# Gates of the dense pair of token blocks: one-hot products replaced by a scattered add into DRAM

## The chip, the cores and the metric

The kernel runs on one core of one Trainium2 chip. The metric is device time in microseconds (us) of one execution; before the change the median of three runs is 5275.13 us.

## The reference, cut to what matters

Two layers work on 768 tokens of width 1024, 256 of context and 512 latent, in six blocks of 128. A layer is a mixer (recurrence and two kinds of attention) and then a retrieval feed-forward over 16384 experts of one neuron each; the last layer does it for the four latent blocks only. The change is in the feed-forward:

```
q = (hb @ wq).reshape(PEER_BLOCK, PEER_HEADS, 2, PEER_DK // 2)
s = jnp.einsum('thpd,hpnd->thpn', q, subkeys)
top_s, top_i = lax.top_k(s, PEER_TOPK)              # 16 of 128, twice a head
best_s, pos = lax.top_k(cand_s, PEER_TOPK)          # 16 of the 16 x 16 sums
idx = jnp.take_along_axis(cand_i, pos, axis=-1)
g = jax.nn.softmax(best_s, axis=-1)
a = gelu(einsum('td,thkd->thk', hb, u_tab[idx]))
out = einsum('thk,thkd->td', g * a, v_tab[idx])
```

Each token chooses 16 experts in each of 8 heads, 128 in all, with a gate for each. Two heads of a token may choose the same expert; their gates then add.

## The kernel before, in words

Five engines run programs of their own, tied by semaphores: PE (matmuls), ACT, DVE, POOL and SP, which issues the large loads. At the end of each stage `stage_end` makes PE, ACT, DVE and POOL wait for one another; SP runs through.

The blocks of a layer go through the feed-forward in two ways. A **gathered** pair of blocks (`gathered_passes`) takes the products with all experts, in 128 chunks of 128 experts: PE makes h times u (`up_gathered`, L1277, split in two fp32r parts for accuracy, or `up_plain`, L1259, every other chunk of layer 0's second pass), ACT applies gelu (L1685) and SP stores the 128 x 128 x 256 result in DRAM (`hx`, L497). For the split chunks ACT copies the high part of u (L1677) and DVE subtracts for the low part (`low_gathered`, L2501). Later POOL gathers for each token its chosen activations (`take_activations`, L671, one instruction for each of the 128 choices of a block, one element for each partition) and its 128 rows of v (`take_row`, L677, 4 KB for each partition), and DVE adds the weighted rows (`add_row`, L2471). In layer 0 one block's rows are added beside the second products pass (`beside_products`), the other three beside the dense stage (`beside_dense`); in layer 1 both beside the dense stage. A plan (`row_plan`) says after which chunk which row is due.

The **dense** pair is the last one, blocks 4 and 5. It makes both products over all 128 chunks: up (L1352), gelu (L1795), times a matrix of gates G (DVE, L2638), down (L1361 plain in layer 0, L1376 split in layer 1). SP streams one ring tile of 1 MB a chunk (u and v), four slots, each free after the down product of its chunk.

G (expert by token, zero where a token has not chosen) is 128 KB a partition of SBUF. It is built in a stage of its own, `gbuild`: for each token DVE makes one-hot matrices of the row and column of its choices (L2598, L2589, L2594), ACT or DVE weighs them with the gate (L1751, L2594), PE multiplies them to the token's 128 x 128 gates (L1331), and ACT copies them to G (L1756). Beside it POOL gathers 64 activations and in layer 0 fetches 3 rows.

The order in a layer: queries of the first pair; its products pass, in which DVE does the top-k work of that pair (`retrieve`, a few steps after each chunk, ready at chunk 44) and at chunk 60 the queries of the next pair; in layer 0 a second products pass (blocks 2, 3) with the queries of blocks 4, 5 after chunk 16 and the added rows of block 0; `gbuild`; the dense stage. In layer 1 there is one products pass (blocks 2, 3). ACT and POOL take part in the choice by the softmax exponent (`gates`) and by storing the gates in DRAM (`gx`, L698). Where indices of one pair would be overwritten they are parked in DRAM (`ix`), and so is the sum of block 0 (`ys`).

## Time and profile before

| | |
|---|---|
| runs | 5266.3, 5275.13, 5329.87 us; median 5275.13 |
| profiled execution | 5303.6 us, span 5301.9 us |
| busy | PE 88%, PE weight load 73%, DVE 59%, POOL 34%, ACT 29% |
| DMA | 1103.74 MB, mean 208 GB/s |

A row by stage gives the busy time of each engine in that stretch, the number of its instructions in brackets, the clock that TensorE was granted (1.00 is full), the mean busy share of the 16 DMA engines and what they moved. The stages of layer 0, by their start in us: queries 810, first products pass 874, second 1331 (queries in it at 1410), build 1945, dense 2063 to 3101; of layer 1: queries 3755, products 3828 (queries in it at 4010), build 4271, dense 4447 to 5280. fp32 matmuls stand as two records each.

### The profile page before, as it was taken

Reading aid. Unit: us, or ns where it says so; the run is one execution under the profiler, and the core shown is the slowest. Engines: PE = TensorE matmul, PEld = TensorE weight load, DVE = VectorE, ACT = ScalarE, POOL = GpSimd, SP = SyncE. Lnnn points to the kernel's source line nnn. Section 1 sums busy time; section 2 is a strip of 40 time slices with the busy share of each in tenths; the row PEclk is TensorE's granted clock in tenths of the full one; section 3 lists DMA queues with packets and bytes.
Section 4 is the critical chain, followed back from the end, with each engine's and each line's share of the span. In section 5 each row is a group of like instructions: output and inputs, shape, how many; then the busy total and the mean of one; then the engine's idle time right before and its main releaser. Section 6 shows DMA issues by size and latency. Waiting matters only on the chain.

```text
span 5301.9 us, 75651 instructions
## 1 busy us (share of the span) xinstructions
PE 4666.2 (88%) x25798; PEld 3895.4 (73%) x25798; DVE 3121.5 (59%) x6247; ACT 1525.4 (29%) x2757; POOL 1827.7 (34%) x1918
## 2 busy tenths in 40 slices
PE   8889899999788876898998987799999948999998
PEld 6569788999777765555555665588899947778886
DVE  2673646666356656454554655646576736667777
ACT  2333422534212233000000023334253425222322
POOL 1111210000456557666666411113000041666652
PEclk9989999999889989999999998799999969999999
DMA  4331115656479863888998942212365722889997
GB/s 150 112 104 54 31 72 177 223 176 211 145 259 321 304 219 123 316 320 317 335 334 330 371 173 79 79 62 66 131 215 177 226 77 76 318 321 339 359 356 267
DMA packets 316699, 1103.74 MB, mean 208 GB/s; under 512 B 59392, under 2 KB 108672, under 8 KB 267872
## 3 DMA queue, kind: packets, MB, share of 16 engines
q1 hardware_dynamic: 165024, 648.09, 35.1%
q0 software_dynamic: 151488, 453.35, 23.9%
q8 instruction: 93, 1.52, 0.1%
q14 instruction: 94, 0.77, 0.0%
HBM read 1037.13 MB, written 62.03 MB: 207 GB/s over the span
## 4 chain that ended last, share of the span: by engine, by line
PE 69%; issue 9%; another core or an unknown queue 7%; DVE 7%; ACT 4%; POOL 2%; POOLq 1%; DMA 1%; ACTq 0%; DVEq 0%; PEldq 0%; SPq 0%
PE PS L1277 16%; PE PS L1352 14%; PE PS L1361 7%; PE PS L1376 6%; PE PS L1222 5%; PE PS L939 3%; PE PS L937 3%; PE PS L1259 3%; PE PS L1180 3%; PE PS L1019 2%; POOL arena L671 1%; PE PS L998 1%; DVE PS L2471 1%; PE PS L1076 1%
## 5 line engine op out<-in xcount | busy, mean ns | idle before, releaser
L1277 PE MATMUL PS<-hS,wS 128*128 128x256 f32 x7680 | 974.5, 289 | 92.4 <-ACT wS L1677 69.1
L1277 PEld LDWEIGHTS PS<-hS,wS 128*128 128x128 f32 x7680 | 954.2, 196 | 109.4 <-issue 80.4
L671 POOL DMA_INDIRECT arena<-hx,arena x768 | 788.5, 1027 | 630.6 <-POOLq L406 333.0
L1352 PE MATMUL PS<-hS,ring 128*128 128x256 f32 x4096 | 954.4, 384 | 51.5 <-issue 41.4
L1352 PEld LDWEIGHTS PS<-hS,ring 128*128 128x128 f32 x4096 | 786.4, 192 | 233.2 <-issue 119.4
L2501 DVE TENSOR_TENSOR wS<-ring,wS 128x1024 fp32r<-128x1024 f32 x320 | 392.0, 1225 | 469.0 <-ACT wS L1677 382.3
L677 POOL DMA_INDIRECT arena<-in_experts,arena x465 | 480.7, 1034 | 515.1 <-DVE PS L2471 392.5
L2471 DVE SCALAR_TENSOR_TENSOR PS<-arena,PS 128x1024 f32<-128x1024 f32 x462 | 593.4, 1284 | 26.3 <-DMA arena<-in_experts,arena 13.2
L1361 PE MATMUL PS<-ring,arena 128*128 128x512 f32 x1024 | 488.1, 622 | 61.2 <-DVE arena L2638 53.8
L1795 ACT ACTIVATE arena<-PS 128x256 f32<-128x256 f32 x256 | 97.3, 384 | 1280.7 <-PE PS L1352 776.9
L2638 DVE TENSOR_TENSOR arena<-arena 128x256 f32<-128x256 f32 x256 | 108.8, 425 | 533.8 <-ACT arena L1795 354.6
L1376 PE MATMUL PS<-wS,gS_ 128*128 128x512 f32 x1536 | 403.1, 412 | 16.0 <-DVE gS_ L2642 13.1
L1361 PEld LDWEIGHTS PS<-ring,arena 128*128 128x128 f32 x1024 | 202.9, 200 | 276.7 <-issue 208.8
L2471 DVE SCALAR_TENSOR_TENSOR PS<-spare,arena,PS 128x1024 f32<-128x1024 f32 x300 | 385.9, 1286 | 28.0 <-DMA spare<-in_experts,arena 6.4
L1685 ACT ACTIVATE arena<-PS 128x256 f32<-128x256 f32 x384 | 147.5, 384 | 787.6 <-PE PS L1277 466.9
L677 POOL DMA_INDIRECT spare<-in_experts,arena x303 | 291.9, 963 | 217.7 <-DVE PS L2471 141.3
L1376 PEld LDWEIGHTS PS<-wS,gS_ 128*128 128x128 f32 x1536 | 292.8, 191 | 83.0 <-DVE gS_ L2642 15.9
L1677 ACT ACTIVATE wS<-ring 128x1024 fp32r<-128x1024 f32 x320 | 336.6, 1052 | 11.3 <-DMA ring<-in_experts 8.2
L1259 PE MATMUL PS<-arena,ring 128*128 128x256 f32 x1024 | 246.0, 392 | 31.4 <-issue 21.2
L1259 PEld LDWEIGHTS PS<-arena,ring 128*128 128x128 f32 x1024 | 195.9, 197 | 65.0 <-issue 27.7
L1222 PE MATMUL PS<-arena,ring 128*128 128x256 f32 x1024 | 230.4, 384 | 11.8 <-DMA ring<-in_wq 11.8
L698 POOL DMA_DIRECT2D gx<-arena x6 | 3.4, 568 | 673.3 <-DVE arena L2111 377.3
(331 smaller groups left out, 6299.4 us busy)
## 6 DMA issues: line engine op xcount, KB each, us to landing
ring<-in_experts SPq DMA_DIRECT2D x256, 1024.0 KB
ring<-in_experts SPq DMA_DIRECT2D x384, 512.0 KB
ring<-in_wcat SPq DMA_DIRECT2D x80, 1024.0 KB
hx<-arena SPq DMA_DIRECT2D x384, 128.0 KB
ring<-in_wq SPq DMA_DIRECT2D x40, 1024.0 KB
arena<-in_rpb POOLq DMA_DIRECT2D x96, 128.0 KB, 2.6
arena<-hx,arena POOLq DMA_INDIRECT x768
arena<-xs POOLq DMA_DIRECT2D x20, 512.0 KB, 5.6
```

Of the source, the lines that this page charges most:

```text
L671: pool.indirect_dma_start(out=aX[n][:, k:k + 1], out_offset=None, in_=src, in_offset=bass.IndirectOffsetOnAxis(ap=at[:, k:k + 1], axis=0)) ...
L677: pool.indirect_dma_start(out=dst, out_offset=None, in_=d["experts"].rearrange("l c p (h f) -> (l c p h) f", h=2), in_offset=bass.Indirect ...
L937: return pe.matmul(bank[n % 4][:, 0:end_ - at], w[:, m * P:(m + 1) * P], h[:, k, at:end_], start=start, stop=stop)
L1222: mm = pe.matmul(bank[n % 4][:, 0:PASS], w[:, m, k, :], tokens[:, k, :], start=(k == 0), stop=(k == KD - 1))
L1259: mm = pe.matmul(bank[6 + c % 2][:, 0:PASS], u[:, k, :], hP[:, k, :], start=(k == 0), stop=(k == KD - 1))
L1277: mm = pe.matmul(bank[6 + c % 2][:, 0:PASS], u[:, k, :], hS[:, h, k, :], start=(part == 0 and k == 0), stop=(part == 2 and k == KD - 1))
L1352: mm = pe.matmul(bank[c % 2][:, 0:PASS], u[:, k, :], hS[:, 0, k, :].bitcast(F32), start=(k == 0), stop=(k == KD - 1))
L1361: mm = pe.matmul(bank[4 + 2 * tb + h], gel[2 + c % 2][:, tb * P:(tb + 1) * P], ring[:, sl, D + 512 * h:D + 512 * h + 512], start=start, st ...
L1376: mm = pe.matmul(bank[4 + 2 * tb + h], gS_[:, 2 * (c % 2) + g, tb * P:(tb + 1) * P], wS[:, 2 * (c % 2) + v, 512 * h:512 * h + 512], start= ...
L1677: act.activation(wS[:, 2 * (c % 2) * (per == 1), :], ring[:, c % SLOTS, 0:D], ACT.Copy).then_inc(s["xu_hi"], 1)
L2471: op = dve.scalar_tensor_tensor(out=total, in0=row, scalar=aX[n][:, k:k + 1], in1=total, op0=ALU.mult, op1=ALU.add)
L2501: dve.tensor_tensor(wS[:, at + 1, :], ring[:, c % SLOTS, 0:D], wS[:, at, :].bitcast(F32), ALU.subtract).then_inc(s["slot_free"], 1)
```

## The change

The dense pair becomes the first one asked: blocks 0 and 1 in layer 0, 2 and 3 in layer 1; the gathered passes are the two others (one in layer 1). There is no `gbuild` stage, no one-hot matrix and no G in SBUF.

Its gates go to a matrix `gd` in DRAM (16.8 MB, chunk, expert, token). SP fills it with zeros during attention, 16 DMAs of 1 MB from a zeroed tile. After the choice DVE makes each chosen element's address (`chosen`), and POOL adds the gates there, one indirect DMA with `compute_op=add` for each of 128 choices and 2 blocks (`scatter`): seven of eight heads in layer 0's first products pass and the last in the second, all eight in layer 1's pass. Each head waits for the same block's head before it to have landed. In the dense stage SP loads 128 KB of gates with each ring tile (`Gb`, four slots), and DVE waits for them.

The normalized tokens of the dense pair are kept in DRAM (`hd`) until the dense stage. Those of the first gathered pair are made within the first queries. The retrieval of the dense pair runs at 2.0 steps a chunk instead of 1.25, before chunk 32, where now the next queries stand; the second pass has its queries after chunk 16 as before. Row buffers are free from the start of the dense stage, so the plan is simpler; rows begin after chunk 2 in layer 0 and chunk 9 in layer 1. All activations but the 64 gathered in layer 0's second pass are gathered in the dense stage (320 in layer 0, 256 in layer 1), the first 16 in layer 0 and 40 in layer 1 ahead of the rows. The parking of indices and of one sum in DRAM falls away, and the token blocks lie elsewhere in SBUF.

The diff, cut to its core:

```diff
-    return range(first_block(layer), NB - 2, 2)
+    return range(first_block(layer) + 2, NB, 2)
+def first_pass(layer, f):
+    return f == first_block(layer) + 2
+def queries_at(layer, f):
+    return 8 if first_pass(layer, f) else 4
...
-    return 11 if f == first_block(layer) else 0
-def queries_at(layer, f):
-    return norm_after(layer, f) + 4
+    return queries_at(layer, f) + 2 if f + 2 < NB else None
 def gates_at(layer, f):
-    return queries_at(layer, f) + (10 if f == first_block(layer) else 12)
+    return queries_at(layer, f) + (10 if first_pass(layer, f) else 12)
...
-        G = view(0, PK, PASS)
         KT0 = 32768
-        kT = view(KT0, 3, PASS)
...
+        eD = arena[:, KT0:KT0 + 2 * P].bitcast(U32).rearrange("p (b k) -> p b k", b=2)
+        gD = view(KT0 + 2 * P, 2, P)
+        Gb = view(23552, SLOTS, PASS)
...
+            def dense(l):
+                base = tally["tiles"]
+                def load(i, sl):
+                    sp.dma_start(ring[:, sl, :], d["experts"][l][bass.ds(i * SLOTS + sl, 1), :, :].rearrange("o p f -> p (o f)")
+                                 ).then_inc(w_ready[sl], 16)
+                def gates(i, sl):
+                    sp.dma_start(Gb[:, sl, :], gd[bass.ds(i * (SLOTS * P * PASS) + sl * P * PASS, P * PASS), :]
+                                 .rearrange("(p t) o -> p (t o)", t=PASS)).then_inc(g_in[sl], 16)
...
+                for tb in range(2):
+                    sp.wait_ge(scattered[tb], 16 * P * (l + 1))
+                for sl in range(SLOTS):
+                    gates(0, sl)
+                with sp.Fori(1, PK // SLOTS) as i:
+                    for sl in range(SLOTS):
+                        sp.wait_ge(s["down_done"], i * SLOTS + (l * PK + sl - SLOTS + 1))
+                        load(i, sl)
+                        gates(i, sl)
...
+                sp.wait_ge(s["zeros_made"], l + 1)
+                size, at_unit = PK * P * PASS // 16, (0 if l == 0 else 12 * len(units(0)))
+                for i in range(16):
+                    sp.wait_ge(s["exp_done"], 1 + at_unit + 2 * i)
+                    sp.dma_start(gd[i * size:(i + 1) * size, :].rearrange("(p t) o -> p (t o)", p=64),
+                                 k8[64:128, 0:size // 64]).then_inc(s["zero_out"], 16)
...
+                def scatter(heads):
+                    for h in heads:
+                        for tb in range(2):
+                            if h:
+                                pool.wait_ge(scattered[tb], 16 * (P * l + TOPK * h))
+                            for k in range(TOPK * h, TOPK * (h + 1)):
+                                pool.indirect_dma_start(out=gd, out_offset=bass.IndirectOffsetOnAxis(ap=eD[:, tb, k:k + 1], axis=0),
+                                                        in_=gD[:, tb, k:k + 1], in_offset=None, compute_op=ALU.add
+                                                        ).then_inc(scattered[tb], 16)
...
+                    if first_pass(l, f):
+                        if f + 2 < NB:
+                            pool.wait_ge(s["hd_out"], 16 * (l + 1))
+                            pool.wait_ge(s["pq_done"], 16 * t["pass"])
+                            load_pass(f + 2)
+                        pool.wait_ge(s["gates_ready"], l + 1)
+                        scatter(range(HEADS if l + 1 == DEPTH else HEADS - 1))
                     else:
-                        pool.dma_start(ix[0], eB.rearrange("p b k -> p (b k)")).then_inc(s["ix_out"], 16)
-                        pool.dma_start(ix[1], vB.rearrange("p b k -> p (b k)")).then_inc(s["ix_out"], 16)
+                        store_gates(f - 2)
                         pool.dma_start(gX[3], gx[l, f0]).then_inc(s["gx_in"], 16)
+                        scatter([HEADS - 1])
...
-                built = min(P, ahead + BUILT)
-                take_activations(0, late[0], range(ahead, built))
-                due, buf, prev = row_plan(len(late), buffers_free(l))
-                held = HELD if early else 0
-                for r in range(held):
-                    take_row(vX[l][buf[r]], buf[r], vA[:, late[0] % 2], r)
-                end(f"gbuild{l}{b0}")
...
+                    groups(1, meet, 0)
                     t["tiles"] = base + meet * SLOTS
-                    queries(hQ if some_plain(l, f) else hP)
+                    queries(hP)
...
-                    def gates_of(i, first):
-                        for g in range(GD):
-                            pe.wait_ge(s["row_made" if g % 2 else "rows_ready"], i * (GD // 2) + (gb // 2 + g // 2 + 1))
-                            if not first:
-                                pe.wait_ge(s["g_used"], i * GD + (gb + g + 1 - GD))
-                            for q in range(4):
-                                mm = pe.matmul(bank[4 + g][:, q * P:(q + 1) * P], oneA[g][:, q, :],
-                                               oneB[g][:, q, :].bitcast(F32), start=True, stop=True)
-                            mm.then_inc(s["one_used"], 1)
...
-                    def weigh_group(i, g):
-                        act.wait_ge(s["one_ready"], i * (GD // 2) + (gb // 2 + g // 2 + 1))
-                        if not isinstance(i, int) or i:
-                            act.wait_ge(s["one_used"], i * GD + (gb + g + 1 - GD))
-                        for q in range(4):
-                            at = arena[:, bass.ds(i * (4 * GD) + (KT0 + 2 * PASS + 4 * g + q), 1)]
-                            last = act.activation(oneA[g][:, q, :], oneR[g][:, q, :].bitcast(F32), ACT.Identity, scale=at)
-                        last.then_inc(s["rows_ready"], 1)
-                    def copy_out(i, g):
-                        act.wait_ge(s["one_used"], i * GD + (gb + g + 1))
-                        act.activation(G[:, :, bass.ds(i * (4 * GD) + 4 * g, 4)],
-                                       bank[4 + g].rearrange("p (t j) -> p j t", j=P), ACT.Copy
...
+                for tb in range(2):
+                    act.wait_ge(scattered[tb], 16 * P * (l + 1))
...
+                def chosen():
+                    dve.wait_ge(s["sel_ready"], 2 * t["pass"])
+                    for tb in range(2):
+                        last = dve.scalar_tensor_tensor(out=eXD[:, tb], in0=sels[tb][:, 1, :], scalar=float(P),
+                                                        in1=sels[tb][:, 0, :], op0=ALU.mult, op1=ALU.add)
+                    link(last)
+                    for tb in range(2):
+                        last = dve.tensor_scalar(eFD[:, tb], eXD[:, tb], float(PASS), pcol[:, tb:tb + 1], ALU.mult, ALU.add)
+                    link(last)
+                    for tb in range(2):
+                        dve.tensor_copy(eD[:, tb], eFD[:, tb])
+                        last = dve.tensor_copy(gD[:, tb], sels[tb][:, 2, :])
+                    last.then_inc(s["gates_ready"], 1)
...
-                        own = retrieve(t["pass"], 0, 4 * FIRST_GATES + 1)
...
-                            some_steps(own, c, 1.25)
+                            some_steps(own, c, 2.0)
                         for _ in own:
                             pass
                         t["pass"] += 1
-                        indices(True)
+                        chosen()
...
-                                dve.tensor_tensor(oneB[g], iota[:, :].unsqueeze(1).broadcast_to([P, 4, P]),
-                                                  at[:, 1].unsqueeze(2).broadcast_to([P, 4, P]), ALU.is_equal)
-                                for n in range(4):
-                                    own, gate = (arena[:, bass.ds(i * (4 * GD) + (KT0 + v * PASS + 4 * g + n), 1)]
-                                                 for v in (0, 2))
-                                    last = dve.tensor_scalar(oneA[g][:, n, :], iota[:, :], own, gate,
-                                                             ALU.is_equal, ALU.mult)
...
-                        dve.tensor_tensor(gel[2 + c % 2], gel[c % 2], G[:, c, :], ALU.mult).then_inc(s["gfull"], 1)
...
+                    dve.wait_ge(g_in[c % SLOTS], 16 * (l * PK // SLOTS + c // SLOTS + 1))
+                    dve.tensor_tensor(gel[2 + c % 2], gel[c % 2], Gb[:, c % SLOTS, :], ALU.mult).then_inc(s["gfull"], 1)
...
```

## Rows read from the trace of the kernel before

**Rows 1.** The page: the chain that ended last, by line (share of the span).

```profile
PE PS L1277 16%; PE PS L1352 14%; PE PS L1361 7%; PE PS L1376 6%; PE PS L1222 5%; PE PS L939 3%; PE PS L937 3%; PE PS L1259 3%; PE PS L1180 3%; PE PS L1019 2%; POOL arena L671 1%; PE PS L998 1%; DVE PS L2471 1%; PE PS L1076 1%
```

**Rows 2.** Busy time by stage: us, busy (x instructions) per engine, clock, DMA share, GB/s.

```profile
874.00:1331.00 457.00, 442.94 (x3438) 434.25 (x3438) 317.30 (x869) 214.89 (x318) 6.93 (x12) 0.99 0.65 207
1476.00:1945.00 469.00, 390.79 (x2218) 350.42 (x2217) 284.40 (x410) 97.97 (x171) 262.76 (x257) 0.91 0.86 297
1945.00:2063.00 118.00, 68.75 (x516) 62.32 (x515) 92.41 (x194) 71.99 (x192) 85.00 (x67) 0.92 0.16 56
2063.00:3101.00 1038.00, 938.73 (x3072) 599.41 (x3072) 546.01 (x533) 48.14 (x128) 621.35 (x651) 0.95 0.88 323
3828.00:4271.00 443.00, 434.66 (x3392) 425.72 (x3391) 309.24 (x850) 209.16 (x312) 1.15 (x2) 1.00 0.64 203
4271.00:4447.00 176.00, 74.86 (x512) 68.42 (x512) 91.88 (x193) 72.58 (x192) 64.00 (x64) 0.76 0.09 31
4447.00:5280.00 833.00, 808.27 (x3584) 682.58 (x3584) 572.72 (x652) 233.37 (x384) 477.94 (x456) 0.99 0.87 321
```

**Rows 3.** The same view, three stretches in which PE runs undisturbed.

```profile
2999.00:3051.00 52.00, 52.00 (x182) 34.39 (x181) 35.43 (x35) 2.69 (x7) 22.33 (x23) 1.00 0.98 378
5123.00:5175.00 52.00, 52.00 (x236) 44.37 (x235) 39.48 (x45) 15.96 (x25) 17.63 (x18) 1.00 0.95 348
1126.00:1320.00 194.00, 193.63 (x1614) 193.43 (x1613) 137.80 (x295) 93.25 (x138) 0.00 (x0) 1.00 0.69 219
```

**Rows 4.** Instructions in order of time, PE, layer 0's second pass: start, us, instruction.

```profile
1387.32 3.61 PE L1259 MATMUL PS<-arena,ring 128*128 128x256 f32 x16
1393.64 3.61 PE L1259 MATMUL PS<-arena,ring 128*128 128x256 f32 x16
```

**Rows 5.** Busy time in layer 0's queries of the second pass.

```profile
1410.00:1476.00 66.00, 65.70 (x347) 58.73 (x346) 39.68 (x265) 12.23 (x27) 31.35 (x33) 1.00 0.38 124
```

**Rows 6.** Busy time in two stretches with gathers of single activations.

```profile
1353.00:1378.00 25.00, 5.17 (x18) 3.85 (x18) 2.64 (x3) 3.67 (x6) 12.89 (x14) 0.52 0.13 35
4271.00:4360.00 89.00, 21.90 (x112) 20.20 (x112) 22.72 (x47) 15.24 (x40) 64.00 (x64) 0.58 0.18 61
```

**Rows 7.** Instructions in order of time, PE: last products, first dense ones.

```profile
1938.72 3.61 PE L1259 MATMUL PS<-arena,ring 128*128 128x256 f32 x16
...
2063.09 3.36 PE L1352 MATMUL PS<-hS,ring 128*128 128x256 f32 x7 [8.61 <-POOLq L406]
...
4265.72 4.00 PE L1277 MATMUL PS<-hS,wS 128*128 128x256 f32 x32
...
4447.08 7.17 PE L1352 MATMUL PS<-hS,ring 128*128 128x256 f32 x32 [0.72 <-ACTq L406]
```

**Rows 8.** DMA issues: KB each, us from issue to landing.

```profile
hS<-hQ SPq DMA_DIRECT2D x1, 1024.0 KB, 5.3
```

**Rows 9.** Busy time of layer 1's first pass up to its choice.

```profile
3828.00:3956.00 128.00, 125.73 (x1042) 124.94 (x1042) 106.92 (x265) 71.19 (x99) 0.84 (x2) 1.00 0.70 220
```

**Rows 10.** The page: instructions, busy us, mean ns; idle us, releaser.

```profile
L2501 DVE TENSOR_TENSOR wS<-ring,wS 128x1024 fp32r<-128x1024 f32 x320 | 392.0, 1225 | 469.0 <-ACT wS L1677 382.3
```

**Rows 11.** Busy time in layer 0's attention.

```profile
500.00:716.00 216.00, 188.43 (x1242) 166.13 (x1241) 129.55 (x400) 103.47 (x253) 57.75 (x78) 0.96 0.13 37
```

**Rows 12.** Instructions in order of time, POOL: gathers in the two build stages.

```profile
2000.32 1.63 POOL L671 DMA_INDIRECT arena<-hx,arena  x1 [0.30 <-issue]
...
2003.50 1.60 POOL L671 DMA_INDIRECT arena<-hx,arena  x1 [0.31 <-issue]
...
4308.48 0.95 POOL L671 DMA_INDIRECT arena<-hx,arena  x1 [0.30 <-issue]
4309.73 0.95 POOL L671 DMA_INDIRECT arena<-hx,arena  x1 [0.30 <-issue]
```

**Rows 13.** One line: times ns (min/median/max), first and last start.

```profile
L671 POOL DMA_INDIRECT arena<-hx,arena x768: 946/952/2007, 1328.4 to 5096.8; - x192
...
L677 POOL DMA_INDIRECT arena<-in_experts,arena x465: 937/945/2007, 1476.0 to 5259.6; - x155
```

More of the change, by code:

```diff
@@ L117, in rows_due @@
         for c in range(PK):
-            have = sum(not f or f + lead <= c for f in free)
-            at += min(step, have / 2 + 0.5) if have else 0
+            at += min(step, buffers / 2 + 0.5) if c >= start else 0
             due.append(min(total, int(at)) if c < PK - 1 else total)
@@ L125, in row_plan @@
         step += 1 / 64
[L126 to L135 removed]
+    return rows_due(step), [r % buffers for r in range(total)]
 class Chain:
@@ L316, in build @@
         xl = view(XL, 2, D)
+        hD = view(XL, KD, PASS)
         xf = view(4096, 4, D)
@@ new lines, in group @@
+                def group(i, first, last):
+                    for sl in range(SLOTS):
+                        if sl < SLOTS - 1:
+                            up(i, sl + 1, sl + 1)
+                        elif not last:
+                            up(i + 1, 0, 0)
+                        down(i, sl, sl, first and sl == 0, last and sl == SLOTS - 1)
+                pe.wait_ge(s["h_in"], 16 * (ps_ + 1))
+                up(0, 0, 0)
+                group(0, True, False)
+                with pe.Fori(1, PK // SLOTS - 1) as i:
+                    group(i, False, False)
@@ new lines, in _, with v_high @@
+                ps_ = t.get("dense", 0)
+                cb = ps_ * PK
+                t0 = t["tiles"]
+                sb_ = sum(split_rows(m) for m in range(l)) * PK
+                def v_high(i, c, first=False):
+                    sl = c % SLOTS
+                    act.wait_ge(w_ready[sl], (i + c // SLOTS) * 16 + 16 * (t0 // SLOTS + 1))
+                    if not (first and c < 2):
+                        act.wait_ge(s["down_done"], i * SLOTS + (cb + c - 1))
+                    act.activation(wS[:, 2 * (c % 2), :], ring[:, sl, D:2 * D], ACT.Copy).then_inc(s["v_hi"], 1)
```

707 lines of the change are left out of this document (298 added, 409 removed).

## The prediction

> **What bounds the kernel now.** I read the chain of waits first, then the busy time by stage, then the instructions around each stage boundary. The chain says that TensorE (PE) sets the end: its lines for the gathered products (L1277), the dense up product (L1352) and the dense down products (L1361, L1376) lead it, and no other engine has more than 1% on one line [rows 1]. Cut by stage, PE is nearly full in each layer's first products pass (443 of 457 and 435 of 443 us), less so in layer 0's second pass (391 of 469) and its dense stage (939 of 1038), and almost full in layer 1's dense stage (808 of 833). Between them stand the two gate-building stages, where PE works 69 of 118 us and 75 of 176 us, on one-hot products alone [rows 2]. The critical resource of everything else, PE at its pace, is given by three undisturbed stretches: 182 matmul records in 52 us, 24 to a dense plain chunk, so 6.86 us a chunk; 236 records, 28 to a split chunk, so 6.17 us; 1614 in 194 us, 24 to a gathered chunk, so 2.88 us [rows 3]. A plain and a split chunk of layer 0's second pass take 6.32 us together [rows 4].
>
> Against that pace four stretches lose time, and each of them has POOL gathering single activations (one 4-byte element for each partition) from DRAM: the second pass of layer 0 (1331 to 1942 less 66 us of queries [rows 5] and 64 x 6.32 leaves 141 us, with 192 gathers by the code), layer 0's dense stage (1038 - 128 x 6.86 = 160 us, 256 gathers), layer 1's dense stage (833 - 128 x 6.17 = 43 us, 192 gathers), and the build of layer 1, which takes 58 us longer than that of layer 0 with the same work and the same 64 gathers [rows 2, 6]. In two stretches where POOL issues nothing but such gathers PE does 5.2 of 25 us and 21.9 of 89 us while DMA is 13 to 18% busy [rows 6]. When only row fetches are left, PE loses nothing [rows 3]. So a gather costs 0.73, 0.62, 0.22 and about 0.9 us of PE, and in the build of layer 0 none that I can see. The smaller costs go with a busier VectorE (DVE): 0.61, 0.53, 0.69 of the time, and 0.78 in layer 0's build [rows 2]. Why, the trace does not show; the change adds 512 instructions of this kind.
>
> **The change part by part.**
> *The build stages go.* From the last product to the first dense product it is 1942.3 to 2063.1 and 4269.7 to 4447.1, so 121 + 177 = 298 us [rows 7]. What stays is a boundary: the 1 MB copy of h lands in 5.3 us [rows 8], then the first 1 MB tile (2.8 us at the 378 GB/s of [rows 3]), and some 4 us of barrier, formerly beside the build. The first gate tiles queue behind five megabytes, 14 us, but the first two up products (7 us) run meanwhile. I take 14 us a layer (9 if the barrier hides, 30 at worst, the length of the dead stretch in rows 6). Removed net: 298 - 28 = 270.
>
> *Gate loads.* 128 loads of 128 KB a layer, 16.8 MB. Full DMA is 378 / 0.98 = 386 GB/s, so 44 us of all engines. The dense stages use 0.88 x 1038 = 913 and 0.87 x 833 = 725 us of DMA; with the loads 957 and 769, still below the 0.98 at which PE ran full [rows 2, 3]. Hidden on average, not in every moment: I take 20 us a layer, between 0 and 44. The added DVE wait comes right behind a ring tile issued three chunks, 20 us, earlier; behind it stand the row additions, and PE and ACT wait for its product.
>
> *Gathers that lose their stage.* 64 a layer (and 3 row fetches) move into the dense stages. At those stages' rates 64 x 0.62 + 64 x 0.22 = 54 us; nothing, if the loss goes with the hour and not the gather; I take 27. POOL has room: 704 instructions x 1.32 us = 929 of 1038 us.
>
> *Retrieval pressed together.* The first choice now ends before chunk 32 instead of 44. DVE has 107 us of work in the 128 us to the choice [rows 9], 44 x 1.22 = 54 of it weight splits [rows 10]; the other 53 plus 26 splits (32) and the links between them make about 100 us, where PE wants 26 x 2.88 = 75. PE is slowed for part of it, as it already loses 3 us there: 5 us a layer, 10 together, at most 30, at least 0. The choice then comes 100 us into the pass instead of 128; with 3 us of index arithmetic (eight small instructions) the scatters start at 977 and 3931.
>
> *Scatters.* 256 a layer: 7 heads (224) in layer 0's first pass, 32 in the second, 256 in layer 1's only pass. No row shows a DMA that adds into DRAM. The nearest are the gathers, with the same 128 elements: in the second pass 257 such instructions are 263 us busy plus 0.30 between them, 1.32 us each [rows 2]. Ends: 977 + 224 x 1.32 = 1273, before the pass ends at about 1331 + 5 = 1336; 3931 + 256 x 1.32 = 4269, before 4271 + 5 = 4276. So POOL's issue is covered, narrowly in layer 1; past it every 0.1 us costs 26 us. The waits from head to head have 16 instructions, 21 us, of the other block between them: nothing. The 32 left over (42 us) delay the end of the first 32 gathers from 1373 to 1415, and the next wait for query products that begin at 1410 anyway [rows 5]: nothing. What the scatters do to PE is the disputed term: 0 to 0.73 us each. The first passes have DVE at 0.69 to 0.70, like the dense stage of layer 1 [rows 2], so I take its 0.22: 512 x 0.22 = 113 us, ends 0 and 374.
>
> *Zeros, and the rest.* 16.8 MB a layer are written in attention, where DMA is 13% busy [rows 11]; 44 us in 216, cover enough. SP waits there, with only weight tiles behind it that wait for later slots. Uncovered it would be 44 us a layer. The norm moves from products to queries at equal size; POOL's copy of h and DVE's 3 us of indices replace stores and transposes of the same size: 0.
>
> Sum: 270 - 40 - 27 - 10 - 113 = 80 us off. The profiled execution took 5303.6 us (span 5301.9), 28 above the median of 5275.1; 80 off it is 5224, off the median **5195 us**.
>
> What an adding DMA costs, a page bears on. The Trainium skill, Collectives: The Full Stack (the bandwidth ceiling), says that a reduce needs two source reads, hence twice the read descriptors of a copy. No run here shows it; if it held for POOL's instruction, the sum would be that of rival 3.
>
> **The rivals.**
> 1. *No disturbance*: DVE keeps POOL from crowding, as in layer 0's build. 270 - 77 = 193 off, **5082**. For: PE lost nothing with 32 gathers in the queries at 1410 [rows 5]. Chance 0.22.
> 2. *DVE slows the scatters*: with DVE at 0.78 gathers come 1.59 us apart, without it 1.25 [rows 12]. At 1.59: layer 0 ends at 1333 (covered), layer 1 at 3931 + 407 = 4338 (+62); 193 - 62 = 131 off, **5144**. Chance 0.12. The Trainium skill, GPSIMD Engine Reference (Specifications), states that POOL shares its SBUF interfaces with DVE and contends with DVE instructions of two SBUF inputs; rows 12 agree with it.
> 3. *The scatter is the slower instruction* (the other side): if its busy part doubles, 2 x 1.02 + 0.30 = 2.34 us, POOL ends layer 0's pass at 1501 (+165) and layer 1's at 4530 (+254): 193 - 419, **5501**. It decides where (193 + 359 + 345) / 480 = 1.87 us an instruction is passed, 359 and 345 being the time that the two passes give 480 scatters. For: nothing here shows an add at a DMA's target. Against: an instruction that gathers 4 bytes a partition and one that fetches 4 KB take 0.952 and 0.945 us in the middle [rows 13], so the size of the work hardly shows. Chance 0.13.
> 4. *Heavy disturbance*, 0.73 each: 193 - 374, **5456**. Against: the second pass has less DVE work. Chance 0.12.
> 5. *The dense stages turn DMA-bound*: 88 and 54 instead of 40 and 27, with the 113: 5 off, **5270**. Chance 0.08.
> The change doing something else than it says has no place: the one-hot code is gone.
>
> **How the numbers follow.** The forecast, 5195, has 0.33, its own range 5150 to 5240. Two per cent, about what a measurement of this kernel can tell, is 5170 and 5381. Faster: rival 1, most of 2 and a third of the forecast, 0.41. Slower: rivals 3 and 4 with a small tail, 0.26. Same: 0.33. The range runs from 5060, just under rival 1, to 5410; rivals 3 and 4 lie mostly above it, which leaves out about 0.2.
>
> **What would show it.** Right: no stage between products and dense, the first dense product some 14 us after the last gathered one; scatters 1.3 us apart, done before PE in both first passes; dense stages of 1078 and 860 us; first passes 60 us longer, with PE idle beside an idle DMA. Rival 1: first passes unchanged. Rivals 2 and 3: PE and ACT waiting for POOL at the end of the pass. Wrong altogether if the scatters' completion, not their issue, holds POOL at the head-to-head waits, or if attention grows.

## The result and the profile after

The changed kernel takes **5653.9 us** in the median of four runs (5641.8 to 5666.2) beside 5302.5 us of the kernel before (four runs, 5266.3 to 5337.2): ratio 1.066, 95% interval 1.057 to 1.076. The forecast was 5195, range 5060 to 5410. The profiled executions, 5646.7 and 5303.6 us, are 343 us apart where I had 80 the other way.

The page after. First the chain that ended last, by line, then two of its groups (line, engine, operation, out<-in, count | busy us, mean ns | idle before, releaser):

```profile
POOL gd L709 15%; PE PS L1340 12%; PE PS L1349 6%; PE PS L1364 5%; PE PS L1292 3%; PE PS L937 3%; PE PS L935 3%; PE PS L1274 3%; PE PS L1192 2%; PE PS L1234 2%; PE PS L1031 2%; PE PS L1010 1%; DVE wS L2484 1%; POOLq L401 1%
...
L1340 PE MATMUL PS<-hS,ring 128*128 128x256 f32 x4096 | 1000.1, 393 | 337.5 <-POOLq L401 190.4
...
L709 POOL DMA_INDIRECT gd<-arena x512 | 912.5, 1782 | 439.8 <-DVE arena L2467 281.2
```

The scatter, L709, which did not exist before, now leads the chain that PE's products led [rows 1]. By stage, in the columns of [rows 2]: layer 0's first pass and its tail, its second pass with the queries, its dense stage, layer 1's mixer, pass, tail and dense stage:

```profile
889.00:1349.00 460.00, 444.45 (x3417) 431.50 (x3416) 319.22 (x899) 233.56 (x333) 303.38 (x162) 0.99 0.78 200
1349.00:1478.00 129.00, 0.30 (x1) 0.33 (x2) 2.64 (x2) 3.13 (x3) 102.73 (x67) 0.52 0.27 18
1478.00:2124.00 646.00, 524.27 (x2880) 469.14 (x2879) 334.83 (x691) 140.28 (x233) 382.16 (x354) 0.88 0.74 245
2129.00:3276.00 1147.00, 970.85 (x3072) 613.73 (x3072) 547.18 (x533) 48.29 (x128) 680.61 (x717) 0.91 0.86 310
3276.00:3966.00 690.00, 560.44 (x3359) 476.04 (x3358) 351.46 (x793) 241.38 (x420) 112.37 (x161) 0.88 0.33 97
4042.00:4490.00 448.00, 438.91 (x3384) 426.37 (x3384) 309.32 (x856) 222.24 (x313) 297.92 (x155) 1.00 0.79 202
4490.00:4680.00 190.00, 0.00 (x0) 0.00 (x0) 0.00 (x0) 0.27 (x1) 156.71 (x102) 0.51 0.30 29
4680.00:5624.00 944.00, 842.09 (x3584) 692.39 (x3584) 571.76 (x653) 231.30 (x385) 547.30 (x522) 0.94 0.83 302
```

The passes are as long as before (460 and 448 against 457 and 443), but two stretches of 129 and 190 us follow in which PE, DVE and ACT do nothing and only POOL works. The end of the second one, in order of time:

```profile
4638.81 1.55 POOL L709 DMA_INDIRECT gd<-arena  x1 [0.30 <-issue]
4640.66 1.55 POOL L709 DMA_INDIRECT gd<-arena  x1 [0.30 <-issue]
...
4675.90 1.55 POOL L709 DMA_INDIRECT gd<-arena  x1 [0.30 <-issue]
4678.92 1.75 SPq L456 DMA_DIRECT2D arena<-gd  x4
...
4680.26 4.21 PE L1340 MATMUL PS<-hS,ring 128*128 128x256 f32 x9 [190.41 <-POOLq L401]
```

A scatter is 1.55 us busy and 0.30 apart, 1.85 us with nothing beside it; a gather takes 0.95 and 0.30 [rows 12]. And the dense stages take 1147 and 944 us where they took 1038 and 833 [rows 2].

### The profile page after: what moved, and what is told of

Same layout as the page of the kernel before. It is cut to its first block, busy times and chain, and to the rows that moved or that the text cites. A ratio compares the mean times of both kernels' runs of the same rounds, so it can differ in the third digit from the quotient of the medians.

```text
span 5645.0 us, 72801 instructions
## 1 busy us (share of the span) xinstructions
PE 4630.4 (82%) x24762; PEld 3814.6 (68%) x24762; DVE 2939.8 (52%) x5875; ACT 1437.5 (25%) x2419; POOL 2716.5 (48%) x2422
## 4 chain that ended last, share of the span: by engine, by line
PE 47%; POOL 16%; issue 12%; DVE 10%; another core or an unknown queue 10%; ACT 3%; POOLq 1%; DMA 1%; ACTq 0%; DVEq 0%; PEldq 0%; SPq 0%
POOL gd L709 15%; PE PS L1340 12%; PE PS L1349 6%; PE PS L1364 5%; PE PS L1292 3%; PE PS L937 3%; PE PS L935 3%; PE PS L1274 3%; PE PS L1192 2%; PE PS L1234 2%; PE PS L1031 2%; PE PS L1010 1%; DVE wS L2484 1%; POOLq L401 1%
## 5 line engine op out<-in xcount | busy, mean ns | idle before, releaser
L1340 PE MATMUL PS<-hS,ring 128*128 128x256 f32 x4096 | 1000.1, 393 | 337.5 <-POOLq L401 190.4
L1340 PEld LDWEIGHTS PS<-hS,ring 128*128 128x128 f32 x4096 | 802.4, 197 | 546.1 <-issue 240.1
L1292 PE MATMUL PS<-hS,wS 128*128 128x256 f32 x7680 | 986.4, 290 | 218.1 <-ACT wS L1674 174.1
L709 POOL DMA_INDIRECT gd<-arena x512 | 912.5, 1782 | 439.8 <-DVE arena L2467 281.2
L685 POOL DMA_INDIRECT arena<-hx,arena x768 | 763.7, 994 | 250.0 <-issue 231.7
L2484 DVE TENSOR_TENSOR wS<-ring,wS 128x1024 fp32r<-128x1024 f32 x320 | 392.2, 1225 | 588.1 <-ACT wS L1674 500.7
L2434 DVE SCALAR_TENSOR_TENSOR PS<-arena,PS 128x1024 f32<-128x1024 f32 x465 | 597.3, 1284 | 15.9 <-issue 2.1
L1349 PE MATMUL PS<-ring,arena 128*128 128x512 f32 x1024 | 500.7, 635 | 82.6 <-DVE arena L2583 71.6
L2583 DVE TENSOR_TENSOR arena<-arena 128x256 f32<-128x256 f32 x256 | 108.7, 425 | 705.3 <-ACT arena L1756 520.5
L2434 DVE SCALAR_TENSOR_TENSOR PS<-spare,arena,PS 128x1024 f32<-128x1024 f32 x297 | 382.0, 1286 | 22.4 <-DMA spare<-in_experts,arena 1.0
L2556 DVE TENSOR_TENSOR wS<-ring,wS 128x1024 fp32r<-128x1024 f32 x128 | 156.9, 1226 | 347.2 <-ACT wS L1749 269.0
L1234 PE MATMUL PS<-arena,ring 128*128 128x256 f32 x1280 | 296.8, 389 | 37.2 <-issue 25.5
L1234 PEld LDWEIGHTS PS<-arena,ring 128*128 128x128 f32 x1280 | 246.5, 195 | 75.1 <-issue 42.7
```

Source lines behind the costliest of these rows:

```text
L685: pool.indirect_dma_start(out=aX[n][:, k:k + 1], out_offset=None, in_=src, in_offset=bass.IndirectOffsetOnAxis(ap=at[:, k:k + 1], axis=0)) ...
L709: pool.indirect_dma_start(out=gd, out_offset=bass.IndirectOffsetOnAxis(ap=eD[:, tb, k:k + 1], axis=0), in_=gD[:, tb, k:k + 1], in_offset=N ...
L1234: mm = pe.matmul(bank[n % 4][:, 0:PASS], w[:, m, k, :], tokens[:, k, :], start=(k == 0), stop=(k == KD - 1))
L1292: mm = pe.matmul(bank[6 + c % 2][:, 0:PASS], u[:, k, :], hS[:, h, k, :], start=(part == 0 and k == 0), stop=(part == 2 and k == KD - 1))
L1340: mm = pe.matmul(bank[c % 2][:, 0:PASS], u[:, k, :], hS[:, 0, k, :].bitcast(F32), start=(k == 0), stop=(k == KD - 1))
L1349: mm = pe.matmul(bank[4 + 2 * tb + h], gel[2 + c % 2][:, tb * P:(tb + 1) * P], ring[:, sl, D + 512 * h:D + 512 * h + 512], start=start, st ...
```

## The experiments

Each is the changed kernel with one edit, unless it says otherwise.

**A surprise first: the chips differ.** The experiments ran on five chips. On four of them the kernel before takes 4922 to 4925 us, and the changed one, run on one of these, 5191; on the fifth it takes 5296 and the changed one 5620, about as in the first runs (whose chip may be the same one). I call the four *quiet*, the fifth and that of the first runs *disturbed*, and compare numbers of one chip or of quiet chips. The fifth also spreads more: its 13 runs of the kernel before go from 5233.9 to 5370.6 us.

**r_before, r_after: both kernels on a quiet chip.**

> The kernel before, unchanged, for a profile from the chip of the experiments. There its median was 4923 us instead of 5275. If the excess of the first chip is in the stretches where POOL gathers (second pass, dense stages, build of layer 1), these are 350 us shorter here and the undisturbed first passes, mixers and queries as long as before; the gathers then disturb nothing here. If it is the clock (0.970 against 0.944 granted), all stages are shorter in proportion to PE's share.

> The changed kernel, unchanged, on the chip of the experiments. Theory A alone (tails of 127 and 186 us against the removed 298, and small dense-stage costs that are the same on every chip): 4923 + 20 to 60 us for tails less build, plus gate loads and a longer attention, some 4990 to 5250. Without its 248 gate loads it took 5194 here, so with them it should take 5195 to 5220 if they are hidden, 5250 and more if not.

Measured: 4923.0 us (4916.5 to 4929.6) and 5190.8 (5189.9 to 5194.6), ratio 1.054 (1.052 to 1.056). The kernel before, its second pass behind the queries, dense stage 0, build 1, dense stage 1 on the quiet chip:

```profile
1446.00:1815.00 369.00, 358.95 (x2243) 332.91 (x2242) 284.95 (x415) 102.12 (x172) 276.29 (x259) 1.00 0.99 378
1935.00:2813.00 878.00, 877.82 (x3058) 582.82 (x3059) 548.92 (x533) 49.03 (x128) 613.43 (x651) 1.00 0.98 382
3992.00:4103.00 111.00, 68.46 (x519) 62.20 (x517) 92.58 (x194) 72.33 (x193) 82.03 (x64) 0.97 0.14 49
4103.00:4895.00 792.00, 789.58 (x3561) 672.93 (x3562) 568.89 (x644) 236.02 (x382) 468.67 (x456) 1.00 0.92 338
```

They stand against 469, 1038, 176 and 833 us in [rows 2]. These windows of the quiet chip end some 6 us before the last product of each dense stage; taken from product to product, the four differ by 98, 154, 66 and 31 us, and 25 more lie in the second pass ahead of its queries (53 us here, 78 there). That is 374 of the 375 us between the two profiled spans: the difference between the chips lies in the stretches with gathers and nowhere else. The changed kernel there, dense stage 0, the tail and dense stage 1 of layer 1:

```profile
1998.00:2953.00 955.00, 899.81 (x3056) 577.81 (x3055) 541.22 (x532) 48.80 (x127) 679.20 (x716) 0.99 0.98 372
...
4173.00:4363.00 190.00, 0.00 (x0) 0.00 (x0) 0.00 (x0) 0.34 (x1) 156.83 (x102) 0.51 0.29 29
4363.00:5156.00 793.00, 791.61 (x3561) 674.37 (x3561) 569.05 (x643) 236.02 (x382) 530.39 (x522) 1.00 0.95 359
```

The tail is the same 190 us on either sort of chip; dense stage 1 costs nothing here (793 for 792), dense stage 0 costs 77.

**e1 and e2: the price of the scatter.** In e1 a gather stands in the scatter's place, in e2 the scatter does not add (both on a quiet chip):

```
- indirect_dma_start(out=gd, out_offset=...(eD[:, tb, k:k + 1]), in_=gD[:, tb, k:k + 1], in_offset=None, compute_op=ALU.add)
e1: indirect_dma_start(out=gD[:, tb, k:k + 1], out_offset=None, in_=gd, in_offset=...(eD[:, tb, k:k + 1]))
e2: indirect_dma_start(out=gd, out_offset=...(eD[:, tb, k:k + 1]), in_=gD[:, tb, k:k + 1], in_offset=None)
```

> Each of the 512 adding scatters is replaced by a gather of one element for each partition from the same matrix, by the same indices, into the gate columns (so the gates are never scattered: the dense pair gets gates of zero). Theory A (the scatter is the slower POOL instruction: 1.55 us busy and 0.30 between against 0.95 and 0.30 of a gather): the gathers come 1.25 to 1.35 us apart, POOL ends layer 0's first pass at 996 + 224 x 1.35 = 1298, before the products end at 1349, and layer 1's at 4144 + 256 x 1.35 = 4490 instead of 4677; the tails of 127 and 186 us go, and the kernel takes some 5340 to 5360 us. Rival (POOL's time is the number of DMAs in flight or of completions, whatever their kind): 1.85 us apart and the tails stay, 5640. Second rival (gathers, unlike scatters, disturb the other engines): tails gone, but the two first passes grow by 0.2 to 0.6 us a gather, 100 to 300 us in all, 5450 to 5600.

> The scatters write instead of adding (a gate chosen by two heads for one token is then lost; nothing else changes). If the add is what costs POOL 0.6 us more than a gather, the scatters take 0.95 us and the result is as with gathers, some 5340 to 5360 us. If it is the direction (a scattered write of 128 elements, each a descriptor of its own into DRAM), they stay at 1.55 us and the kernel at 5640 to 5660; the DMA share in the tail (0.22 and 0.29) then falls only if the add costs the DMA engines something.

Measured: 4889.1 us (4887.1 to 4895.1) and 4898.3 (4896.3 to 4902.0), where the changed kernel takes 5190.8: 302 and 293 us off. One line each, times in ns (minimum/median/maximum), e1 and then e2:

```profile
L709 POOL DMA_INDIRECT arena<-gd,arena x512: 944/948/1972, 999.1 to 4056.2; - x171
```

```profile
L709 POOL DMA_INDIRECT gd<-arena x512: 964/971/2004, 996.5 to 4070.3; - x171
```

Of e2, the same stretch as the tail above, from the last product of layer 1 to the first dense one:

```profile
4050.00:4074.00 24.00, 0.02 (x1) 0.02 (x1) 0.00 (x0) 0.04 (x1) 16.38 (x17) 0.58 0.60 230
```

So reading or writing makes no difference (0.95 and 0.97 us); **the addition is what costs POOL 0.58 us more, 1.55 us**, and that takes the stretch from 24 to 190 us. Theory A holds; the direction is out, and so is the number of DMAs in flight. The two forecasts of 5340 to 5360 us were for the first chip, some 300 us off its 5654, and 302 and 293 is what came off on a quiet one.

The page counts the DMA's packets too, here of r_after and then of e2 (e1 has the same numbers of packets as e2):

```profile
DMA packets 429084, 1169.58 MB, mean 225 GB/s; under 512 B 137600, under 2 KB 219648, under 8 KB 377952
```

```profile
DMA packets 371740, 1169.58 MB, mean 239 GB/s; under 512 B 80256, under 2 KB 162304, under 8 KB 320608
```

With the addition there are 57,344 small packets more, 112 for each of the 512 instructions. In stretches with scatters alone the software queue shows some 34 packets for a plain one (542 for 16 in e2) and some 145 for an adding one (13,466 for 93 in r_after). POOL's time and its packets grow together; that the one makes the other no run shows.

**e3: the gate loads.** Of 128 loads a layer four are left (`gates(i, sl)` is taken out of the loop, VectorE waits for the first ones only).

> Only the first four gate tiles of a layer are loaded in the dense stages; the other 124 chunks take old tiles of gates (248 loads of 128 KB, 32.5 MB, are left out, with VectorE's waits for them). Theory B1 (the dense stages are 109 and 111 us longer because of the gate loads on the DMA engines and in SP's queue): they come back to 1040 to 1060 and 835 to 850 us, 5450 to 5480 in all. Theory B2 (they are longer because of the gathers moved into them and the 40 that open layer 1's): 0 to 40 us off, 5610 to 5650, and the first 104 us of layer 1's dense stage still have POOL full and PE at half.

Measured: 5194.3 us (5193.4 to 5195.9), the changed kernel 5190.8: nothing. The loads are hidden on the quiet chip, and B1 is out there. On the disturbed chip e8 below, which keeps all the loads, has dense stages as short as the quiet chip's, so they cost nothing there either.

**e8: the gathers of the dense stages**, on the disturbed chip, beside the unchanged kernel there:

```
- rest = [(n, k) for n in ... for k in range(..., P)]
+ rest = [(n, k) for n in ... for k in range(..., P) if k % 32 == 31]
```

> The changed kernel again, beside the following ones on the same chip: 5191 us if it is the chip of the last runs, 5654 if it is one like the first. In the second case layer 1's dense stage is 931 us long again and not 793, and the following kernel, without most gathers there, tells whether it is the gathers that make it so.

> Of the 320 and 256 gathers of single activations that the dense stages issue, only one in 32 stays (those rows are then weighted with old numbers). Layer 0's dense stage took 955 us against 878 of the kernel before on the same chip, without any gain from leaving the gate loads out. Theory P (POOL is its bound: 704 instructions x 1.35 = 950 us, and VectorE, which makes the gates' products in order behind the row additions, waits for the rows): it comes back to 878 us, PE's pace; layer 1's, with 512 instructions, stays at 793; 5191 - 77 = 5114. Rival (the DMA engines, 0.98 busy, are its bound): 310 gathers of 512 bytes are too little to matter, it stays above 940, and the kernel above 5175.

Measured: 5619.9 us (5611.7 to 5635.7) and 5242.7 (5236.5 to 5260.3), 377 off. Dense stages 0 and 1 of the changed kernel on this chip, then of e8:

```profile
2134.00:3269.00 1135.00, 971.99 (x3057) 612.22 (x3057) 546.80 (x533) 48.17 (x128) 681.76 (x715) 0.90 0.87 313
...
4678.00:5601.00 923.00, 833.42 (x3561) 689.24 (x3560) 562.20 (x643) 231.23 (x383) 552.17 (x522) 0.94 0.85 308
```

```profile
2118.00:2999.00 881.00, 878.12 (x3057) 582.20 (x3056) 548.69 (x532) 48.66 (x127) 378.32 (x406) 1.00 1.01 403
4413.00:5204.00 791.00, 791.00 (x3566) 674.44 (x3565) 569.82 (x644) 236.60 (x384) 269.89 (x274) 1.00 0.95 359
```

Without most gathers the dense stages of the disturbed chip are as short as a quiet chip's (881 for 878, 791 for 792); with them a gather costs 254 / 310 = 0.82 us in layer 0 and 132 / 248 = 0.53 in layer 1. The DMA engines carry more (403 GB/s) when the stage is shorter, and e3's stage 0 is as long as the changed kernel's, 963 us from first to last product, with 16 MB less to move (DMA busy 0.94 instead of 0.97), so they aren't its bound. What the other engines wait for, in dense stage 1 on the disturbed chip, PE (us in total, times, longest):

```profile
PE PS L1340 <- issue: 49.5, 45, 3.6
PE PS L1364 <- DVE gS_ L2587: 26.6, 12, 4.3
PE PS L1364 <- issue: 12.5, 8, 2.9
```

"issue" is idle time in which nothing visible is waited for; on the quiet chip this list has one wait of 1.0 us. For layer 0, 77 of the cost is there on a quiet chip too: POOL is 679 us busy in 716 instructions, with 0.30 between them 894 of 955 us, and VectorE makes the gates' products (L2583) in order behind the row additions (L2434), which wait for POOL's rows. What PE and VectorE wait for there, on the quiet chip (r_after):

```profile
PE PS L1349 <- DVE arena L2583: 54.9, 49, 9.5
```

```profile
DVE PS L2434 <- DMA spare<-in_experts,arena: 283.1, 165, 5.2
```

In 67 us POOL itself waits for VectorE to free a row buffer, so the two hold each other up, POOL far more. e9b and e13 below have 16 gathers fewer in this stage and take 947 and 943 us from first to last product instead of 963, 1.0 to 1.2 us an instruction. Theory P holds, for layer 0; its own test, e8, fell on the disturbed chip, where it takes off this bound and the disturbance together.

**e4: the zeros.** Layer 1's 16 transfers are left out (its dense pair then also has layer 0's gates).

> The zero fill of layer 1 (16 transfers of 1 MB in attention) is left out; the matrix then holds layer 0's gates too, so that layer 1's dense pair is wrong. If the fill made attention longer (layer 1's mixer took 690 us instead of 654), that stage comes back to about 655 us and the kernel is 30 to 36 us faster than the changed one. If it was hidden, nothing changes (within 5 us).

Measured: 5169.3 us (5166.3 to 5173.0), 21.5 off, neither of the two forecasts. I had put the zeros at nothing behind attention.

**e5: the kernel before, its gathers moved** (BUILT is 64 in layer 0 and 0 in layer 1, `head = 40`), on a quiet chip.

> The kernel before, with layer 1's 64 gathers of the build stage issued at the start of the dense stage (40 of them ahead of the first row instead of 16): everything else as before. If gathers slow the other engines wherever they are, the build of layer 1 shrinks from 176 to about 118 us, that of layer 0, and its dense stage grows by 50 to 60 us from 833: nothing in all, 5260 to 5310. If the dense stage hides them, 50 to 60 us are gained, 5215 to 5250, and theory B2 for the changed kernel is wrong. If the build stage was long for another reason, it stays at 176 and the whole becomes 10 to 50 us slower.

Measured: 4946.4 us (4943.2 to 4948.4) beside 4923.1, ratio 1.004 (1.003 to 1.006). None of the three, for the forecasts were for the first chip: the build stays as it was (110 us), since on a quiet chip it never suffered, and the dense stage takes 13 us more. In the profiled execution 6 us more stand before layer 0's first queries, where nothing was changed. What the move does on a disturbed chip isn't known.

**e7: layer 0's scatters divided 5 to 3** (`range(HEADS - 3)` in the first pass, the others in the second).

> Layer 0's scatters are divided 5 heads to the first pass and 3 to the second, instead of 7 and 1. At 2.0 to 2.3 us each beside a busy VectorE, the 160 scatters end at 996 + 160 x 2.15 = 1340, before the products (1349): layer 0's tail of 127 us goes. The 64 moved ones take 120 to 140 us at the head of the second pass, where POOL has its gathers and rows later: if POOL has slack there, the kernel gains 100 to 127 us; if the second pass is then bound by POOL's row fetches (0.95 us each and VectorE's 1.29), up to all of it is given back there and the kernel stays within 20 us.

Measured: 5195.7 us (5189.0 to 5196.4), nothing gained. The tail goes, the second pass becomes as much longer (519 us behind its queries instead of 396): POOL has no slack to move work into.

**e9 to e13: can it be had without the addition?** VectorE sums the gates of a token's repeated experts, and plain scatters write head by head, all 8 heads in the first pass; 80 gathers ahead instead of 64 (in the second pass, beside the 128 of the block whose rows are added there).

```
+ def merge(h, tb):            # n = TOPK * (h + 1)
+     for e in range(TOPK * h, TOPK * (h + 1)):
+         scalar_tensor_tensor(out=both[...], in0=eK[:, tb, 0:n], scalar=eK[:, tb, e:e + 1], in1=gR[:, tb, 0:n],
+                              op0=ALU.is_equal, op1=ALU.mult, accum_out=gD[:, tb, e:e + 1])
```

> A version meant to be right and fast: VectorE gives each choice of a head the sum of its own gate and those of earlier heads for the same expert (224 small instructions a layer, some 30 us, in sixteens between the chunks), so that a plain scatter, the last writer winning, does what the adding one did. All 8 heads are scattered in the first pass of layer 0 too, and 80 instead of 64 gathers are taken ahead in its second pass. By the plain scatter's 0.97 us busy, POOL ends at 1000 + 256 x 1.27 = 1325 in layer 0, before the products. Expected from 4898 us of the plain scatters: 10 us less for the 32 scatters out of the second pass, up to 20 less for the 16 gathers out of the dense stage, 0 to 30 more for VectorE: 4870 to 4920, level with the kernel before or 1% faster.

> The merged version again. On a disturbed chip 5766 and a first pass of 485 us in layer 1, as before. On an undisturbed one 4870 to 4920, level with the kernel before or 1% faster, with that pass at 283 to 300.

> The same with 112 gathers taken ahead in layer 0's second pass instead of 80. If both stages are bound by POOL's count of instructions (1.3 us each), 32 x 1.35 = 43 us go from the dense stage to the second pass and the kernel stays where it is, within 10 us; if the second pass still has slack, it is up to 40 us faster.

Measured: on the disturbed chip 5765.9 us (5758.5 to 5782.8) and, with 112 ahead, 5771.7 (5741.7 to 5785.9), the same as forecast: what the dense stage gains the second pass loses. Both are slower even than the adding scatters' 5619.9. On a quiet chip 5001.3 (4999.8 to 5006.5). The rest of layer 1's pass behind the queries, of the changed kernel on the disturbed chip, of e9 there, and of e9b on the quiet one:

```profile
4204.00:4487.00 283.00, 280.28 (x2310) 277.50 (x2308) 175.26 (x330) 164.69 (x221) 245.25 (x122) 1.00 0.88 217
```

```profile
4316.00:4801.00 485.00, 334.93 (x2304) 315.70 (x2302) 229.65 (x777) 163.43 (x220) 252.25 (x224) 0.79 0.42 127
```

```profile
3803.00:4116.00 313.00, 288.50 (x2310) 282.74 (x2308) 229.86 (x778) 164.64 (x221) 228.10 (x187) 0.98 0.65 197
```

The sums cost 30 us of this pass (313 for 283 on the quiet chip); the other 172 are the plain scatters on the disturbed chip, which the adding ones don't cost there. That it is the scatters and not the sums, two stretches at the end of e9's pass show. Both are without sums, the first has the last 27 scatters and the second none:

```profile
4700.00:4737.00 37.00, 23.78 (x146) 21.55 (x146) 6.95 (x6) 9.32 (x12) 28.54 (x27) 0.77 0.38 113
4737.00:4801.00 64.00, 60.11 (x463) 58.71 (x463) 24.93 (x27) 36.73 (x48) 0.00 (x0) 0.92 0.54 172
```

PE in e9, in order of time: two instructions or one, then idle, for nothing that shows:

```profile
4567.07 0.60 PE L1294 MATMUL PS<-hS,wS 128*128 128x256 f32 x2 [0.64 <-issue]
4569.18 0.60 PE L1294 MATMUL PS<-hS,wS 128*128 128x256 f32 x2 [1.51 <-issue]
4571.31 0.37 PE L1294 MATMUL PS<-hS,wS 128*128 128x256 f32 x1 [1.53 <-issue]
```

POOL's waits in e9b, from 3780 us on, behind the scatters of layer 1's first head, show the second fault, the first sum that came after the second queries:

```profile
POOL gd L713 <- issue: 59.1, 182, 3.9
POOL gd L713 <- DVEq L2485: 46.7, 1, 46.7
```

e13 makes the sums of the second and third heads right behind the choice:

> The merged version with the sums for the second and third heads made right behind the first choice, while VectorE waits for the second queries, and the rest every six chunks. On an undisturbed chip: POOL waited 47 us a layer for the first sums, and VectorE's 75 us of sums a layer made layer 1's pass 29 us longer; both waits go and a third of the sums leaves the pass: 5001 - 94 - 20 = 4887, at worst 4930; 0.5% either side of the kernel before. On a disturbed chip some 5700, far slower than the kernel before there.

Measured, on a quiet chip: 4920.9 us (4915.1 to 4930.7) beside 4922.3, ratio 0.9999 (0.9989 to 1.0008). It draws level with the kernel before, 34 us short of the 4887 that was forecast: POOL's wait goes (9 us from the last product of layer 1 to the first dense one, 56 in e9b), but the rest of the pass stays at 313 us with a third of the sums taken out.

**e11 and e12: is it the pace?** A memset of 512 columns on POOL (0.55 us) behind each plain scatter of e9, and behind each gather of dense stage 1 of the changed kernel.

> The merged version with a memset of 512 columns on POOL behind each plain scatter, which puts them some 1.9 us apart. On a chip of the disturbed kind: if the pace is what starves the other engines, layer 1's first pass comes back from 485 + 8 us to 283 plus a tail of about 150 (433 in all), and the same in layer 0; if it is the plain scatter as such, the pass stays near 480 and gets a tail as well. On an undisturbed chip the tails alone show, 100 to 300 us more than e9b.

> The changed kernel with such a memset behind each of the 256 gathers of layer 1's dense stage. On a disturbed chip that stage took 931 and 923 us, 790 without the gathers: POOL needs 256 x 1.27 + 256 x 1.95 = 824 us now, so with no disturbance left it takes 825 to 850; if the gathers as such disturb, it stays at 920 to 1000. On an undisturbed chip 793 becomes about 825.

Both fell on quiet chips, and e12 again when repeated, so the question stays open. There e11 takes 5165.5 us (ratio 1.050, 1.048 to 1.052), 164 more than e9b, as forecast, and e12 5275.5 (1.072, 1.070 to 1.073; repeated, 5270.8): 85 us more than the changed kernel. Its dense stage 1 takes 877 us where 825 was forecast. POOL is 681 us busy in 778 instructions, has 108 us between its DMAs and waits 78 for VectorE to free row buffers, which the forecast had left out:

```profile
4363.00:5240.00 877.00, 815.23 (x3561) 678.98 (x3560) 560.97 (x643) 221.62 (x382) 681.15 (x778) 0.98 0.89 324
```

e1 ran a second time too, on a quiet chip again (4886.0 us), so what gathers would do to the first passes of a disturbed one isn't known.

## Why the prediction was wrong

The sum had 80 off; the profiled executions have 343 more. Term by term, for the disturbed chip unless another is named:

1. *The build stages go, 270.* Right. Layer 0's boundary is 9 us (from 121), and layer 1's is 24 us where POOL is in time (e2), from 177: 265.
2. *Scatters, the issue: nothing.* **This is the step that failed.** It took a gather's 1.32 us, "covered, narrowly"; the measured instruction is 1.85 us alone and longer while the other engines work: 122 of them take the 283 us of layer 1's pass behind the queries, 2.3 each. Over a whole pass it is 2.1 us (256 from 4144 to 4677 us), past the 1.87 from which rival 3 was to decide. Cost: 129 us in layer 0 and 190 - 24 = 166 in layer 1, 295 in all; e1 and e2 confirm it with 302 and 293. Rival 3 was the right mechanism, with 2.34 us for an instruction where it is 2.1; its sign, PE and ACT waiting for POOL at the end of the pass, is what the rows show. Its price was a guess, though: an adding scatter is 1.55 us busy alone, where I had doubled 1.02, and the rest of the 2.3 comes while the other engines work. That it is VectorE among them, as in rival 2, no run isolates. The argument against it, that the size of the work hardly shows [rows 13], compared two instructions that don't add. The Trainium skill, Collectives: The Full Stack (the bandwidth ceiling), says that a reduce takes two source reads and so twice the read descriptors of a copy; the adding instruction keeps POOL busy 1.6 times as long as the plain one (1.55 against 0.97 us), on that side but short of twice. The packets of the profile, some 145 against 34, grow by far more than twice.
3. *Scatters, the disturbance: 113.* Nothing: PE is full in both passes (439 of 448, 444 of 460). The adding instruction, of all, doesn't disturb on either sort of chip, while plain ones on a disturbed chip do (e9). The 0.22 to 0.73 us that I had read for a gather are no property of the gather alone: on a quiet chip PE is full beside the same gathers (878 of 878 us).
4. *Gate loads 40.* Nothing (e3).
5. *Gathers that lose their stage, 27.* The dense stages grew by 109 and 111 us. "POOL has room" was wrong in layer 0, where its 717 instructions bound the stage even on a quiet chip (77 us); the rest is the disturbance, at (254 - 77) / 310 = 0.57 and 0.53 us a gather instead of my 0.62 and 0.22 (e8), an estimate for layer 0, since the bound and the disturbance may overlap. In layer 1, 59 of the 111 are lost in the first 104 us, where 40 gathers come in a row: 199 matmul records where the kernel before has 466, at the 236 in 52 us of [rows 3]:

```profile
4680.00:4784.00 104.00, 58.43 (x199) 43.01 (x200) 15.67 (x22) 13.72 (x22) 59.70 (x63) 0.68 0.35 114
```

6. *The 32 scatters left for the second pass: nothing.* The queries and the pass take 646 us from the end of the tail where they took 614 from the end of the first pass, 32 more. By the first and last plain product the pass grows by 27 us here and by 22 on the quiet chips, and there with plain scatters in their place (e2) by 6: the adding instruction again.
7. *Zeros: nothing.* Attention grew, which I had named as a sign of being wrong altogether: the two mixers take 13 and 36 us more. In layer 1, 21.5 us of it are the zeros (e4); the 13 of layer 0 and the rest of the 36 no run explains.
8. *Retrieval pressed, 10.* The passes grew by 3 and 5: right.

-265 + 295 + 220 + 32 + 49 + 8 is +339, of 343. On the quiet chips, where no gather disturbs, the change still costs 268 (263 between the profiled spans). The builds were 121 and 111 us there, so only 199 go; 291 come for the two waits for scatters, 79 for dense stage 0, 22 for the second pass, 50 for the mixers and 18 for the rest, 261 in all. The first three of these costs, terms 2, 5 (layer 0) and 6, are **POOL's time**. Even with scatters at the plain one's price (e2) the change gains only 25 us there, 4898.3 for 4923.1, and not the 193 of rival 1. I had cost POOL's additions one by one against the slack of each stage, with a price borrowed from another instruction, and the disputed term that I priced most carefully (3) was the wrong one.

## What to carry to other kernels

When work is moved onto a queue that issues one instruction for 128 elements, count its instructions stage by stage at a measured price of that very instruction; if a cover is "narrow", the price is the forecast. Replacing dense one-hot products by scatters took away two stages of 298 us together, in which PE was busy for 144, and gave POOL 912 us of work, and a version tuned to hide it (e13) only drew level. And a kernel's stage may be slower on one chip than on another for one sort of instruction: compare two kernels on the same chip.

## What was not expected of the hardware

- An indirect DMA that adds into DRAM keeps POOL 1.55 us for 128 elements; the same without the addition 0.97, a gather 0.95. The addition brings 112 small packets more for each instruction.
- On one of five chips, and in the first runs, PE, ACT and VectorE stand idle without a visible reason while POOL issues gathers or plain scatters every 1.27 us: 350 us of the kernel before. In the traces of this kernel and the changed one from two of the other four (r_before, r_after) PE has no such wait of more than 2.1 us. Whether the pace decides was tried on quiet chips only; what sets the two sorts apart is open.
- A VectorE instruction of 32 to 128 columns that also sums takes 0.30 us and 0.08 to read the sum; 224 of them keep it busy for 56.4 + 18.6 = 75 us, not the 30 that I had put for them.
